# Samples' attention over pages: a unit's weights are transposed ahead of the turning of later keys instead of behind it

## The reference, cut to what matters

```
s_past = einsum('bqhc,bkc->bhqk', q_lat, ckv_past) + einsum('bqhr,bkr->bhqk', q_pe, kpe_past)
p      = softmax(concatenate([s_past, s_new], -1) * MLA_SCALE, -1)
o_lat  = einsum('bhqk,bkc->bqhc', p[..., :P], ckv_past) + einsum('bhqk,bkc->bqhc', p[..., P:], ckv_new)
```

## Time and profile before

| what | value |
|---|---|
| median of 3 runs | 2535.82 us (2533.68 to 2535.89) |
| the profiled execution, its own time | 2536.45 us |
| span of the profiled execution | 2534.8 us |
| instructions | 35841 |
| TensorE busy | 2208.2 us (87%) |
| weight loads busy | 1990.0 us (79%) |
| VectorE, ScalarE, GpSimd busy | 713.9, 515.2, 242.6 us |
| mean granted clock of TensorE | 0.901 |

### The profile page before, as it was taken

One profiled execution on the slowest core, in us unless ns is written; L12 is line 12 of the kernel. 1 busy time (PEld: TensorE's weight loads), 2 busy tenths in 40 slices (PEclk: granted clock), 3 DMA queues, 4 the chain that ended last, 5 costly groups with the idle time before them and its releaser, 6 DMA issues.

```text
span 2534.8 us, 35841 instructions
## 1 busy us (share of the span) xinstructions
PE 2208.2 (87%) x14774; PEld 1990.0 (79%) x14774; DVE 713.9 (28%) x1347; ACT 515.2 (20%) x1094; POOL 242.6 (10%) x325
## 2 busy tenths in 40 slices
PE   5899898976769999997898699997699999999992
PEld 4788787864659999996654576686699999999991
DVE  2245555537232222222234344402100000000003
ACT  1133422203022212211123233301211111111101
POOL 0000101020002302300020023200100000000001
PEclk8899999956789999998898689977799999999996
DMA  7222100030213242332070256510788988898883
GB/s 192 69 67 75 35 1 4 1 95 26 83 33 92 72 113 76 88 103 71 15 245 1 67 193 237 179 50 1 202 216 211 267 211 211 208 271 215 209 203 123
DMA packets 452952, 306.17 MB, mean 121 GB/s; under 512 B 22381, under 2 KB 435456, under 8 KB 448704
## 3 DMA queue, kind: packets, MB, share of 16 engines
q1 hardware_dynamic: 433812, 225.76, 34.2%
q0 software_dynamic: 19024, 78.72, 9.4%
HBM read 276.44 MB, written 28.14 MB: 120 GB/s over the span
## 4 chain that ended last, share of the span: by engine, by line
PE 66%; issue 19%; DVE 6%; POOL 4%; DMA 2%; SPq 1%; ACT 1%; POOLq 0%; DVEq 0%; ACTq 0%
PE bank L1197 17%; PE bank L526 13%; PE bank L1226 8%; PE bank L1038 3%; POOL actL L2220 2%; PE bank L706 2%; PE bank L691 1%; PE bank L701 1%; PE bank L1052 1%; PE bank L1079 1%; PE bank L564 1%; POOL actH L2217 1%; SPq L2311 1%; PE bank L857 1%; PE bank L859 1%
## 5 line engine op out<-in xcount | busy, mean ns | idle before, releaser
L1197 PE MATMUL bank<-arena,w_ring 128*128 128x176 f32 x2816 | 424.4, 314 | 4.8 <-issue 4.8
L1197 PEld LDWEIGHTS bank<-arena,w_ring 128*128 128x128 f32 x2816 | 422.3, 191 | 6.8 <-issue 6.8
L526 PE MATMUL bank<-hT,w_ring 128*128 128x260 f32 x1600 | 362.8, 389 | 16.2 <-DVE hT L1249 15.1
L526 PEld LDWEIGHTS bank<-hT,w_ring 128*128 128x128 f32 x1600 | 309.3, 194 | 66.0 <-DVE hT L1249 16.0
L1790 ACT ACTIVATE arena<-bank 128x512 f32<-128x512 f32 (+5 forms) x284 | 135.7, 494 | 511.5 <-PE bank L526 225.6
L1226 PE MATMUL bank<-arena 128*128 128x176 f32 x1408 | 220.1, 313 | 0.0
L1226 PEld LDWEIGHTS bank<-arena 128*128 128x128 f32 x1408 | 210.2, 190 | 0.2
L857 PE MATMUL bank<-hH,gu_high 128*128 128x260 f32 x704 | 143.6, 286 | 18.3 <-DVE w_low L1508 18.3
L1752 DVE TENSOR_TENSOR arena<-arena,bank 128x176 f32<-128x176 f32 x88 | 29.8, 338 | 431.6 <-PE bank L1197 431.6
L859 PE MATMUL bank<-hL,gu_high 128*128 128x260 f32 x704 | 143.0, 285 | 0.0
L861 PE MATMUL bank<-hH,w_low 128*128 128x260 f32 x704 | 142.9, 285 | 0.0
(11 more groups left out here) (440 smaller groups left out, 2884.6 us busy)
## 6 DMA issues: line engine op xcount, KB each, us to landing
w_ring<-in_we_gate SPq DMA_DIRECT2D x88, 512.0 KB, 7.2
w_ring<-in_we_up SPq DMA_DIRECT2D x88, 512.0 KB, 7.3
arena<-in_we_down SPq DMA_DIRECT2D x64, 704.0 KB, 6.6
w_ring<-in_w_in_a SPq DMA_DIRECT2D x26, 512.0 KB, 3.8
w_ring<-in_w_gate SPq DMA_DIRECT2D x22, 512.0 KB, 3.9
w_ring<-in_w_up SPq DMA_DIRECT2D x22, 512.0 KB, 3.9
arena<-in_w_down SPq DMA_DIRECT2D x16, 704.0 KB, 6.2
slots<-arena POOLq DMA_DIRECT2D x4, 2560.0 KB
```

The costliest lines, as they stand in the source:

```text
L526: mm = pe.matmul(out[i][:, 0:hi - lo], w_ring[:, s, kt, :], rhs[:, kt, lo:hi], start=(kt == 0), stop=(kt == KT - 1))
L1197: mm = pe.matmul(bank[bk][:, 0:SLOTS], w_ring[:, s, kt, :], hTe[:, kt, :], start=(kt == 0), stop=(kt == KT - 1))
```

## The change

TensorE's step becomes: score_group(G), in an even step turn_weights, then turn_group(G+2), then value_group(G-2). VectorE's step becomes: the copy into `PT` in an even step, the maximum in an odd step, then its copies of group G+2. No instruction is added or removed, and no bank, buffer or semaphore is changed.

```
             for G in range(GROUPS + 2):
+                if G < GROUPS:
+                    score_group(G)
+                if G >= 2 and G % 2 == 0:
+                    turn_weights(G // 2 - 1)
                 if G + TAHEAD < GROUPS:
                     turn_group(G + TAHEAD)
-                if G < GROUPS:
-                    score_group(G)
                 if G >= 2:
-                    if G % 2 == 0:
-                        turn_weights(G // 2 - 1)
                     value_group(G - 2)
...
             for G in range(GROUPS + 2):
-                if G + TAHEAD < GROUPS:
-                    turned(G + TAHEAD)
                 u = G // 2
+                if G >= 2 and G % 2 == 0:
+                    b = filled(dve, ("pt", u - 1))
+                    if u >= 3:
+                        dve.wait_ge(groups_used, 2 * (u - 2))
+                    dve.tensor_copy(PT[:, (u - 1) % 2, :], b).then_inc(free(("pt", u - 1)), 1)
                 if G < GROUPS and G % 2:
...
-                if G >= 2 and G % 2 == 0:
-                    b = filled(dve, ("pt", u - 1))
-                    if u >= 3:
-                        dve.wait_ge(groups_used, 2 * (u - 2))
-                    dve.tensor_copy(PT[:, (u - 1) % 2, :], b).then_inc(free(("pt", u - 1)), 1)
+                if G + TAHEAD < GROUPS:
+                    turned(G + TAHEAD)
```

## The result

The changed kernel takes 2549.72 us, the median of five runs (2545.28 to 2552.38), beside 2535.42 us (2533.68 to 2535.89) for the kernel before in the same series: a ratio of 1.0058 with a 95% interval of 1.0043 to 1.0073. The forecast was 2521.8 us with a range up to 2528. The profiled execution took 2549.72 us, so its span can be set beside the median directly.

The account below looks back on a forecast made before the run. TensorE bounds the stage, idling 0.79 us per two steps for VectorE's copy into `PT`. Saving 1.00 us in each of 14 units, edges 0, takes 14.0 us off the median 2535.82: 2521.8 us, range 2519 to 2528.

Parts of the forecast that it names:

- the sentence on GpSimd's fetches: GpSimd's page fetches in the changed stage, released by the values: 5.7 us to landing, pages needed 20 us later, no cost.
- The prediction's last sentence: What would make the forecast wrong: an unseen stall at the fourth or fifth bank of an even step's group transposes.
- Score to turn: TensorE, from start of score matmuls to start of the next group's transposes, new order: 1.43 us.
- weights to turn: TensorE, even step, from start of the four weight transposes to the group's transposes: 0.51 us.
- values to score: TensorE, from start of value matmuls to start of the next step's score matmuls: 0.86 us.
- the even turn: TensorE, even step, the group's transposes up to the value matmuls: 2.53 us plus a new bank stall of 0.10.
- Two steps: An odd and an even step of the changed stage together: 10.25 us after 11.25, 1.00 saved, 14 times.
- the edges: Stage's first steps: a 0.43 us excess in step 2 against an exponential late by 0.1 to 0.3; counted 0.
- The clock: Rival: TensorE falls to half clock in runs of 24 transposes, net 17 us slower, 2553 us; chance 0.02.
- the exponential: Rival: TensorE waits for ScalarE's exponential at the weight transposes, 4.9 us slower, 2540.7 us; chance 0.03.
- Nothing behind the stage gave time back: Rival: later stretches return the gain, or VectorE's new order stalls as long as the old; 2535.8 us, chance 0.06.
- The rival of the banks: Rival: the wait moves to the transposes' three banks behind VectorE's late copies; gain only 8.4 us, 2527.4 us, chance 0.12.

## Why the prediction was wrong

**The step that failed** is the sentence on GpSimd's fetches: "released by the values, which stay last in the step ... No cost." I asked when the pages are needed (20 us later) and what the DMA share would be, and both answers held (the median to landing is still 5.7 us, the share 0.50). I didn't ask what stands beside the 2.2 us (0.95 + 0.31 + 0.96) in which GpSimd makes the two requests. Released by the values, they begin when the next step does, and the change put the scores there in place of the turn. The prediction's last sentence did name the fourth bank as the place of a stall that it might not see, but in an even turn and from VectorE's copies; it came in odd turns as well, behind idle readers. Measured price: 196.6 - 167.3 = 29.3 us over 24 fetches, 1.2 us each, more than twice the gain that I forecast.

**Everything else in the sum held**, as the run with the later fetch shows, which has the change and not the collision. Score to turn 1.41 (forecast 1.43; 1561.64 less 1560.23 there, as 1566.22 less 1564.81 in the changed kernel), weights to turn 0.50 (0.51), values to score 0.89 (0.86), the even turn 2.56 with its bank stall (2.63). Two steps 10.19 (10.25), so 1.06 us saved per unit and 14 x 1.06 = 14.8. The stage lost 183.6 - 167.3 = 16.3; the other 1.5, by this subtraction, lie at the edges, which I had counted at 0, though I had the 0.43 of step 2 in hand. That kernel's 2521.17 us stands beside the forecast 2521.8; the kernel before took 2537.89 in its series, so the gain is 16.7 us where 14.0 was forecast.

**The rivals.** The clock stayed at 1.00, and the exponential didn't become the wait. Nothing behind the stage gave time back. The rival of the banks is instructive: its sign appeared as I had described it, TensorE waiting at line 1038 for line 1625, but not its cause. It was to come from VectorE's load, and in the profile VectorE sat idle for 2.66 us and more before the late instruction. That difference, a releaser that was itself idle, told the two apart. No rival had the mechanism that decided, and the chance of 0.05 for slower was too small because every case in it lay on the path that the diff names.

**What is shown and what isn't.** Shown: the loss needs an indirect DMA's requests made by GpSimd beside the scores (the fetch moved away, taken out, given to SyncE or replaced by copies: no loss; put there in the old order: the same loss). Shown too: the values' signals are held as well, most of the loss needs two requests in a row, and the signals come bunched. Only argued: that the array itself goes on meanwhile, from the bunching. Open: by which path the making of requests holds signals back, whether a plain DMA of GpSimd does it too, and why transposes beside the same requests are held only when they follow scores that are (before, and in the run with the later fetch, they are read on time). Scores and values differ from transposes in more than their 32 columns, and no run parts these.

## What to carry to other kernels

When an order is changed, write down for every queue what stands beside each of its instructions before and after, not only when it is released and when it is needed: here nothing of GpSimd's moved in its own order, and its neighbour changed. A wait's releaser in the list is a cause only if it was busy; if it was idle and started late behind the end of what it reads, look one step further back, and at what else began in that gap. The repair is one wait: the change with the fetch behind the next scores is 0.63% faster than the kernel before, and as good with the fetch over the values (0.64%) or with only the rotary keys' request over the scores (0.61%).

## What was not expected of the hardware

While GpSimd makes two indirect-DMA requests (0.95 us each, 0.3 apart), the signals behind 32-column matmuls come 1.1 to 1.8 us late, with one alone 0.4, with the second one beside the values 0.6; with plain DMAs issued by SyncE at that place, or 2.65 us of GpSimd copies, they come on time. The Trainium skill, "SBUF — State Buffer", section "Who interferes with whom", states that DMA never contends with a compute engine and that PE and ACT never wait on anyone. No run here shows TensorE's array standing still, but its signals were late by these amounts, and 29.3 us of this stage hung on it.

TensorE's rows don't show such a delay: their ends are modelled, and in the changed kernel they run on smoothly through the scores and twelve transposes. It is seen in the starts of idle readers, in the times at which semaphores were raised, or with an idle engine set to watch the signals.
